# The end of the expert phases: one late tile's pair rows weighed by VectorE instead of TensorE

## The reference, cut to what matters

```python
top_p, top_i = lax.top_k(jax.nn.softmax(e_logit, axis=-1), TOP_K)          # TOP_K = 2
top_w = top_p / jnp.sum(top_p, axis=-1, keepdims=True) * g_w
...
    hidden = jax.nn.silu(t @ w1_e) * (t @ w3_e)
    return acc + c_e[:, None] * (hidden @ w2_e), None
...
x = x + mx[5] * y[:n_lat].reshape(x.shape)
return rmsnorm(x, norm_final)
```

## Time and profile before

| what | value |
|---|---|
| median of three runs | 999.28 us (997.64 to 1002.12) |
| the profiled execution's own time | 999.59 us |
| its span, first to last instruction | 997.8 us |
| mean granted TensorE clock over the span | 0.987 |
| PE busy, of the span | 936.5 us (94%) |
| DVE busy | 428.2 us (43%) |
| ACT busy | 247.3 us (25%) |
| chain that ended last: PE / DMA / DVE | 77% / 12% / 4% |

### The profile page before, as it was taken

How to read it: one execution, slowest core, us unless ns; L and a number is a source line. 1 busy time by engine, 2 the same in 40 slices (tenths; PEclk the granted TensorE clock), 3 DMA queues, 4 the chain that set the end, 5 groups by cost and what they waited for, 6 DMA issues and landing times.

```text
span 997.8 us, 17238 instructions
## 1 busy us (share of the span) xinstructions
PE 936.5 (94%) x5859; PEld 592.1 (59%) x5860; DVE 428.2 (43%) x906; ACT 247.3 (25%) x538; POOL 224.9 (23%) x309
## 2 busy tenths in 40 slices
PE   5999999999998999998988899999988999999986
PEld 3444448657886555554555475887875555555552
DVE  3399995487456011110101489556344212222124
ACT  4220102465243222221212340132133111111112
POOL 1017801110003333331421000000003333333310
PEclk9999999999997999998999999999999999999999
DMA  9979325899357899999999999883658999999995
GB/s 345 391 207 367 96 74 194 262 327 366 123 183 252 322 407 405 407 406 408 407 404 408 322 391 386 257 327 98 204 173 283 401 400 408 406 404 402 402 407 233
DMA packets 129948, 315.86 MB, mean 317 GB/s; under 512 B 28987, under 2 KB 60755, under 8 KB 129860
## 3 DMA queue, kind: packets, MB, share of 16 engines
q1 hardware_dynamic: 114152, 295.93, 79.7%
q0 software_dynamic: 10800, 12.72, 3.7%
q10 hardware_dynamic: 4908, 6.03, 1.7%
HBM read 315.00 MB, written 22.31 MB: 338 GB/s over the span
## 4 chain that ended last, share of the span: by engine, by line
PE 77%; DMA 12%; DVE 4%; issue 3%; SPq 2%; ACT 2%; POOLq 0%; POOL 0%; DVEq 0%; ACTq 0%
PE ps L1243 19%; PE ps L1043 17%; PE ps L1269 9%; DMA ring<-in_moe_w 8%; PE ps L1095 8%; PE ps L1053 6%; PE ps L1211 3%; PE ps L975 2%; PE ps L1253 2%; DMA RH<-hrow,sidx_all 1%; PE ps L1420 1%; SPq L761 1%; DMA ring<-in_w_mod 1%; PE ps L1471 1%; PE ps L1502 1%
## 5 line engine op out<-in xcount | busy, mean ns | idle before, releaser
L1243 PE MATMUL ps<-ring,RT 128*64 128x256 f32 x2096 | 252.7, 389 | 18.4 <-DMA ring<-in_moe_w 15.6
L1243 PEld LDWEIGHTS ps<-ring,RT 128*64 128x64 f32 x2096 | 157.1, 140 | 86.6 <-issue 18.8
L1043 PE MATMUL ps<-RT,ring 128*128 128x512 f32 (+1 forms) x544 | 182.1, 493 | 1.1 <-DVE RT L2518 1.1
L1043 PEld LDWEIGHTS ps<-RT,ring 128*128 128x128 f32 x544 | 102.2, 190 | 77.2 <-issue 70.6
L2395 DVE TENSOR_TENSOR RT<-RT,ps 64x256 f32<-64x256 f32 x64 | 27.1, 423 | 259.7 <-ACT RT L1844 152.0
L1269 PE MATMUL ps<-ring,RT 128*64 128x512 f32 x424 | 100.3, 593 | 2.1 <-DVE RT L2401 1.8
L1844 ACT ACTIVATE RT<-ps 64x256 f32<-64x256 f32 x64 | 24.2, 378 | 245.9 <-PE ps L1243 225.6
L2565 DVE SCALAR_TENSOR_TENSOR RAB<-RM,chan,RAB 128x512 f32<-128x512 f32 x120 | 82.3, 768 | 0.0
L2830 POOL DMA_INDIRECT pair_out<-RH,sidx_all x62 | 63.2, 1019 | 55.4 <-POOL sidx_all L2827 49.1
L2806 POOL DMA_INDIRECT RH<-hrow,idx x7 | 8.2, 1171 | 292.9 <-DMA hrow<-RH 191.3
L2818 POOL DMA_INDIRECT RH<-hrow,sidx_all x56 | 59.3, 1060 | 49.4 <-issue 29.1
(11 more groups left out here) (320 smaller groups left out, 1060.1 us busy)
## 6 DMA issues: line engine op xcount, KB each, us to landing
ring<-in_moe_w SPq DMA_DIRECT2D x354, 512.0 KB
ring<-in_w_mod SPq DMA_DIRECT2D x96, 512.0 KB
ring<-in_odd_w_in SPq DMA_DIRECT2D x24, 512.0 KB
ring<-in_even_w_in SPq DMA_DIRECT2D x20, 512.0 KB
ring<-in_even_w_out SPq DMA_DIRECT2D x8, 512.0 KB
RAB<-in_moe_w SPq DMA_DIRECT2D x8, 512.0 KB, 7.6
RAB<-pair_out SPq DMA_DIRECT2D x8, 512.0 KB, 8.5
ring<-in_odd_w_out SPq DMA_DIRECT2D x8, 512.0 KB
```

The costliest lines, as they stand in the source:

```text
L1043: mm = pe.matmul(bank, w[:, c, P * ft:P * (ft + 1)], moving[:, c, :], start=(c == 0), stop=(c == NCH - 1))
L1243: mm = pe.matmul(bank[CAP * k:CAP * (k + 1), 0:BLK], xt(c), rows_at(w[k], c), start=(c == 0), stop=(c == NCH - 1))
```

## The change

Of the first late tile (tile 1) alone:

- PE makes no diagonal products any more, in either layer; its banks hold the late rows only and are closed by the product of expert 31.
- In layer 0, DVE weighs and adds the two pair rows itself, in place (`pair_weighted`, both halves), at the start of `late_pair`, ahead of the first bank. The bank is then added by a plain tensor_tensor.
- In layer 1, DVE adds both weighted pair rows to X (`both_added`): half 0 ahead of expert 31's `gated_y`, half 1 behind it.
- The wait ahead of the ten idle products is for the tenth update of X instead of the eleventh.

```diff
--- before.py
+++ after.py
@@ -1364,9 +1364,15 @@
                             pe.wait_ge(y_ready, n0 + expert + 1)
                             for h in (0, 1):
                                 p = slice(CAP * h, CAP * (h + 1))
+                                last = t == LATE_TILES[0] and e == len(LATE) - 1
                                 mm = pe.matmul(banks[t, h], late_T[p, t, e, :], YS[p, expert % 2, :],
-                                               start=(e == 0), stop=False)
-                                freed(mm)
+                                               start=(e == 0), stop=last)
+                                if last:
+                                    close(mm)
+                                else:
+                                    freed(mm)
+                        if t == LATE_TILES[0]:
+                            continue
                         for h in (0, 1):
                             pe.wait_ge(y_back[t][h], 16 * (l + 1))
                             close(pe.matmul(banks[t, h], first_weight[:, t, :], back[t][:, D * h:D * h + 512],
@@ -1644,7 +1650,7 @@
                     if ft == 1:
                         free(1)
 
-            pe.wait_ge(x_updated, xu_moe[0] - 5)
+            pe.wait_ge(x_updated, xu_moe[0] - 6)
             warm(("xT", LATENT, 0), 10)
             stream_T(LATENT)
             for b in (0, 1):
@@ -2471,13 +2477,37 @@
                     gated_y(LAST_GROUP, 2)
                 copy_hT(LAST_GROUP, 3)
                 if l == 1:
+                    both_added(LATE_TILES[0], 0)
                     gated_y(LAST_GROUP, 3)
 
+            def both_added(t, h):
+
+
+                half = slice(512 * h, 512 * (h + 1))
+                dve.wait_ge(y_back[t][h], 32)
+                for k in (1, 0):
+                    step(dve.scalar_tensor_tensor(out=X[:, t, half], in0=back[t][:, D * h + 512 * k:D * h + 512 * (k + 1)],
+                                                  scalar=topw[:, t, k:k + 1], in1=X[:, t, half],
+                                                  op0=ALU.mult, op1=ALU.add))
+
+            def pair_weighted(t, h):
+
+
+                a, b = back[t][:, D * h:D * h + 512], back[t][:, D * h + 512:D * (h + 1)]
+                dve.wait_ge(y_back[t][h], 16)
+                step(dve.tensor_scalar(b, b, topw[:, t, 1:2], None, ALU.mult))
+                step(dve.scalar_tensor_tensor(out=b, in0=a, scalar=topw[:, t, 0:1], in1=b, op0=ALU.mult, op1=ALU.add))
+
             def late_pair(l):
 
 
+                if l == 1:
+                    both_added(LATE_TILES[0], 1)
+                else:
+                    for h in (0, 1):
+                        pair_weighted(LATE_TILES[0], h)
                 for t in LATE_TILES:
-                    if l == 1:
+                    if l == 1 and t != LATE_TILES[0]:
                         for h in (0, 1):
                             half = slice(512 * h, 512 * (h + 1))
                             dve.wait_ge(y_back[t][h], 32)
@@ -2492,8 +2522,11 @@
                             continue
                         b = back[t][:, D * h + 512:D * (h + 1)]
                         dve.wait_ge(y_back[t][h], 16)
-                        done(dve.scalar_tensor_tensor(out=b, in0=b, scalar=topw[:, t, 1:2], in1=bank,
-                                                      op0=ALU.mult, op1=ALU.add))
+                        if t == LATE_TILES[0]:
+                            done(dve.tensor_tensor(b, b, bank, ALU.add))
+                        else:
+                            done(dve.scalar_tensor_tensor(out=b, in0=b, scalar=topw[:, t, 1:2], in1=bank,
+                                                          op0=ALU.mult, op1=ALU.add))
                         drained(dve, "late", 0, t, h)
                         gate_loaded(dve, 0, 5)
                         step(dve.tensor_tensor(b, b, G[:, t // 2, half], ALU.mult))
```

## The result

The changed kernel takes 1002.2 us (median of 21 runs, 1000.22 to 1003.91); the kernel before, in 21 runs beside it, 1000.31 us (997.64 to 1003.56). The ratio is 1.002 [1.0012, 1.0028]: 2 us slower, clear of zero and well under the 0.5% at which this document speaks of a difference. The profiled execution of the changed kernel took 1001.8 us, with a span of 1000.0 us, 2.2 us more than before's 997.8.

What follows compares the result with a forecast made beforehand. It took DVE's train of late halves to bound layer 0's end and PE to bound layer 1's. The sum was 999.59 + 0.9 + 1.0 - 1.05 = 1000.4 us, range 997.3 to 1003.8.

Steps and rivals of the forecast that it cites:

- The two stretches outside the two ends: Up to layer 0's L1269, and layer 1 from L1043 to its last L1269: predicted change 0 each.
- Which engine bounds where: DVE's train of four late halves sets layer 0's end; in layer 1 PE sets it before, DVE after the change.
- The added weighing, plus 0.9: Layer 0: DVE's weighing of half 1 ends at 561.1, so the train starts later; plus 0.9 us, ends 0.8 and 1.2.
- list of signs: What the new profile would show, such as layer 0's first bank addition about 1.0 us after half 1 has landed.
- The removed products of layer 0, nothing: Layer 0: PE loses two diagonal products and the first bank closes at 559.0; worth nothing, since DVE comes at 561.1.
- The looser wait, nothing: Layer 0: waiting for X's tenth update gains nothing, since the drain of bank 4 holds the idle products.
- the idle products do begin sooner: Layer 0 rival: idle products released by the second update, about 565.4, clock fall irrelevant; 998.0 us, chance 0.05.
- The clock, plus 1.0: Layer 0: half clock after a gap of 4.8 us slows the idle products; plus 1.0 us, ends 0 and 4.2.
- Layer 1, minus 1.05: Layer 1's end: tile 0's last addition begins at 989.7 instead of 990.77; minus 1.05 us, ends minus 1.75 and minus 0.25.
- the burst at half: Layer 0 rival: all twenty idle records run at half clock, plus 4.2 us, 1003.6 us in all; chance 0.17.
- the long half clock: Rival from 568.2 us on: half clock outlasts the idle products into transposes and projections, 1004.5 us; chance 0.04.
- room for the weighing in DVE's wait: Layer 0 rival: rows land 2 us sooner, both weighings vanish in DVE's wait, gaining 1.0; 997.5 us, chance 0.08.

Runs made afterwards that it cites:

- clock_held: Changed kernel plus ten more idle products in an empty bank, without a wait, straight behind the late products: 998.98 us, 1.0002 of the kernel before.
- rows_sooner: Changed kernel with several other loads on SP's queue issued behind the pair rows instead of ahead, in both layers: 999.94 us, 1.0004 of the kernel before.
- act_queue: Changed kernel with tile 1's two loads of layer 0 issued from ACT's queue instead of SP's: 1004.14 us, 1.0042 of the kernel before.
- after_free_bank: Changed kernel with the ten idle products writing to an empty bank, so only the wait for X holds them: 998.77 us, 0.9984 of the kernel before.
- layer1_alone: Only layer 1's half of the change, with layer 0 and its idle products as in the kernel before: 998.92 us, 0.9994 of the kernel before.
- rows_sooner_busy: Changed kernel with SP's loads reordered and fourteen idle products in the empty bank without a wait: 994.15 us, 0.9949 of the kernel before.
- best_act_queue: Changed kernel with idle products in the empty bank and tile 1's loads from ACT's queue in both layers: 1006.41 us, 1.0070 of the kernel before.

## Why the prediction was right, point by point

The range of 997.3 to 1003.8 us was wide enough for most of the rivals too, so that the time fell inside it says little. What bears the prediction out is the terms. The two stretches outside the two ends, which it put at nothing, came to -0.69 and +0.39 us and partly cancelled, which is luck.

- **Which engine bounds where**: right. The idle products are released by DVE's last bank in layer 0, and DVE took over from PE as the bound in layer 1.
- **The added weighing, plus 0.9**: right in kind, 1.22 measured. The landing sets the first bank: in the profiles of four kernels with the second half landed at 557.7, 558.2 (`clock_held`), 559.3 and 564.1, the bank is added 1.4 to 1.5 us later. The forecast had 1.29 for a weighing (and 1.0 in its list of signs, which does not follow from its sum) and left out some 0.1 us between landing and first instruction; the loads landed some 0.2 us later against L1269 than before (4.86 instead of 4.67), which makes up the rest. In the executions of the changed kernel and of `clock_held` there is a tie that the working did not see: in the first, half 0 is weighed at 559.29, just as half 1 lands. In `rows_sooner` and `act_queue` DVE waits for half 1 alone (1.06 and 0.86 us), so these two show that its landing sets the bank.
- **The removed products of layer 0, nothing**: right; their bank lay ready 2.5 us (558.2 to 560.67). What they did cost lies in the clock's term: PE is done 8.57 us after L1269 (563.01) instead of 9.62 (564.75), which is 1.05 of the 2.28 us by which the gap grew.
- **The looser wait, nothing**: right, and shown by `after_free_bank`, which takes the other wait away. The rival that the idle products do begin sooner fell as a reading of the change, and became true when the bank was changed: it was priced at 1.6 us under the kernel before, and that kernel came out 1.6 [0.3, 2.9] us under. In part by other ways than the rival named, since there the clock fell all the same.
- **The clock, plus 1.0**: the term that was mis-sized. It was put between 0 and 4.2, and the lower value taken because the old kernel's executions were to pay a part of it too. For this nothing was found: in both profiles with the old layer 0 and the old idle products (before, `layer1_alone`) these took 4.55 us at full clock; of the other executions only the mean clock over the span is known. It measured 2.44 us in the profile, about the middle. The stretch at half began at 566.0, as worked out (565.8), and lasted 6.7 us. With this term at 2.4 and the others as they were, the sum would have been 1001.8, the changed kernel's own time. The Trainium skill (TensorE: Matmul & The Clock Gate, "Why this matters for your kernels") says that idleness between bursts of products puts the clock back to its half level. The trace agrees: the clock fell in the gap of 4.83 us. That the whole burst would then run at half was the prediction's reading of it, and did not come, as the clock was back at full 4.9 us into the burst.
- **Layer 1, minus 1.05**: right, 1.24 in the profile; the delay of `gated_y` was 0.72 us where 0.7 was worked out. Most of the 0.2 us more is in the two bank additions of tile 1, which take 1.29 us now that both banks lie ready; the working kept the 1.48 us of the row before, where DVE was waiting for PE's banks. The runs alone do not resolve it.
- **The rivals**: neither the burst at half nor the long half clock came; the clock was full again at 572.8, inside the burst. That there is room for the weighing in DVE's wait was false here, and stayed half false even in `rows_sooner`, whose rows land 1.1 us earlier against L1273: the room is what is left of the wait behind the landing. In `rows_sooner_busy` it is there in layer 1.

One theory of the experiments fell. The rows were to come sooner from another queue; they did not. What helped, in layer 0, was to issue less ahead of them. That it is the bytes ahead which count, and not the order on the queue as such, fits these runs but was not tried by itself.

Not tried: weighing only half 0 on DVE and leaving half 1 to PE, which would keep the weighing clear of the second landing.

## What to carry to other kernels

Idle time of an engine is room for added work only from the moment the work's operands are there: look up the landing inside the wait, and count only what remains behind it. Of several waits in front of an instruction the last one binds, so loosening another changes nothing until that one is moved too. And work taken off PE ahead of a wait becomes a longer gap, which can cost more through the clock than the work did; idle products that wait for nothing, in a bank that is free, gave it back.

## What the runs showed of the hardware

- **The length of the gap alone does not tell whether the clock falls.** It stayed full around gaps of 2.55 and 2.45 us (before, `layer1_alone`). It fell around one of 1.85 us in `after_free_bank` (half from 566.0 to 569.3), and around one of 2.33 us in the kernel before itself. Waits just ahead of the gap do not decide it alone: in `after_free_bank` PE had waited 0.45 and 0.24 us for rows among its last products, but ahead of the gap of 2.33 us it had worked from 441.90 to 448.36 without a wait (timeline of PE, 440 to 458 us), as it had from 557.00 to 564.75 ahead of the one of 2.55 us. What decides is open.
- **The price hardly grows with the gap.** Twenty idle records took 6.81, 6.74, 6.99, 7.53 and 7.00 us behind gaps of 4.34 (`best_act_queue`), 4.73, 4.83, 4.83 and 7.52 us (`act_queue`), and 6.24 us behind the gap of 1.85, against 4.48 us with no gap.
- **A load on another queue was no faster here.** In layer 0 the two halves took 7.4 and 9.1 us to landing from ACT's queue, issued 3.9 us later in the span (554.6, 550.7); 7.3 and 8.2 from SP's; 5.3 and 7.2 from SP's with fewer loads issued ahead.
